# Recurrent stage: one triangular inverse by blocks for both directions, log of beta in the exponent, recurrence steps that follow as chunks end

## The reference, cut to what matters

```python
g    = -exp(a_log) * softplus(a + dt_bias)      # log decay, one per token, head and direction
beta = sigmoid(b)                               # one per token, head and direction
gc   = cumsum(g) within the chunk
gam  = exp(gc_i - gc_j) for j <= i, else 0
a_kk = strict_lower( (k*beta) @ k.T * gam )
u, w = solve (a_kk + I) [u | w] = [v*beta | k*beta*exp(gc)]      # unit lower triangular
a_qk = (q @ k.T) * gam
for every chunk, in order of time:
    v_new = u - w @ state
    o     = (q * exp(gc)) @ state + a_qk @ v_new
    state = state * exp(g_last) + (k * exp(g_last - gc)).T @ v_new
```

## Time and profile before

| | us |
|---|---|
| median of 3 runs (lowest, highest) | 2108.91 (2108.44, 2112.96) |
| the profiled execution's own time | 2110.14 |
| its span in the profile | 2108.3 |
| PE busy | 1998.5 (95%) |
| DVE, ACT, POOL busy | 940.0, 743.6, 614.7 |
| first and last PE record of the gdn stage start at | 212.71, before 546.32 |

### The profile page before, as it was taken

How to read it: one execution, slowest core, us unless ns; L and a number is a source line. 1 busy time by engine, 2 the same in 40 slices (tenths; PEclk the granted TensorE clock), 3 DMA queues, 4 the chain that set the end, 5 groups by cost and what they waited for, 6 DMA issues and landing times.

```text
span 2108.3 us, 25286 instructions
## 1 busy us (share of the span) xinstructions
PE 1998.5 (95%) x10748; PEld 1607.1 (76%) x10748; DVE 940.0 (45%) x1549; ACT 743.6 (35%) x1235; POOL 614.7 (29%) x206
## 2 busy tenths in 40 slices
PE   6998899999999999999999999998999999999997
PEld 3777899999977787778778888887766548766456
DVE  4797455656522221303336403514534664434663
ACT  4674232221433322322233212223343553343551
POOL 2431211222432322334424444442423002423001
PEclk8999799999999999999999999998999999999999
DMA  4121000000233322322222222221312002212001
GB/s 170 60 80 60 1 1 2 2 1 1 95 120 105 106 90 76 111 84 91 89 80 82 98 100 100 100 99 61 130 60 80 1 1 83 90 60 80 1 1 40
DMA packets 29001, 142.01 MB, mean 67 GB/s; under 512 B 2871, under 2 KB 7351, under 8 KB 14808
## 3 DMA queue, kind: packets, MB, share of 16 engines
q1 hardware_dynamic: 18944, 123.27, 16.5%
q10 hardware_dynamic: 9944, 17.12, 2.5%
HBM read 135.13 MB, written 5.24 MB: 67 GB/s over the span
## 4 chain that ended last, share of the span: by engine, by line
PE 86%; DVE 7%; ACT 4%; issue 1%; DMA 0%; POOL 0%; SPq 0%; POOLq 0%; DVEq 0%; ACTq 0%
PE bank L398 48%; PE bank L942 13%; PE bank L599 4%; PE bank L409 3%; PE bank L1800 3%; PE bank L1821 3%; PE bank L1807 2%; DVE WK L868 2%; PE bank L957 2%; PE bank L1275 1%; DVE WK L887 1%; PE bank L1251 1%; PE bank L1749 1%; ACT WK L1930 1%; ACT w_part L356 1%
## 5 line engine op out<-in xcount | busy, mean ns | idle before, releaser
L398 PE MATMUL bank<-x_part,w_part 128*128 128x512 f32 x3360 | 786.7, 394 | 3.5 <-ACT WK L1497 3.0
L398 PEld LDWEIGHTS bank<-x_part,w_part 128*128 128x128 f32 x3360 | 633.1, 189 | 141.5 <-issue 9.0
L2240 POOL TENSOR_TENSOR w_part<-RAW,w_part 128x2048 fp32r<-128x2048 f32 (+1 forms) x90 | 403.3, 4484 | 780.1 <-ACT w_part L356 777.7
L942 PE MATMUL bank<-WK 128*128 128x64 f32 (+1 forms) x2336 | 281.2, 277 | 3.4 <-DVE WK L1088 1.6
L942 PEld LDWEIGHTS bank<-WK 128*128 128x128 f32 x2336 | 275.7, 195 | 4.3 <-DVE WK L1088 1.8
L2240 POOL TENSOR_TENSOR w_part<-WK,w_part 128x2048 fp32r<-128x2048 f32 (+1 forms) x30 | 126.2, 4206 | 376.5 <-ACT w_part L356 376.5
L356 ACT ACTIVATE w_part<-RAW 128x2048 fp32r<-128x2048 f32 (+1 forms) x90 | 166.4, 1850 | 173.9 <-PE bank L398 138.3
L398 PE MATMUL bank<-f_part,w_part 128*128 128x512 f32 x768 | 174.4, 389 | 0.0
L398 PEld LDWEIGHTS bank<-f_part,w_part 128*128 128x128 f32 x768 | 144.2, 188 | 29.9
L868 DVE SCALAR_TENSOR_TENSOR WK<-WK,COL 128x512 f32<-128x512 f32 x96 | 101.7, 1060 | 3.4
L1009 ACT ACTIVATE WK<-bank 128x256 f32<-128x256 f32 x80 | 31.0, 388 | 200.9 <-PE bank L957 200.6
(11 more groups left out here) (257 smaller groups left out, 2372.6 us busy)
## 6 DMA issues: line engine op xcount, KB each, us to landing
RAW<-wts SPq DMA_DIRECT2D x84, 1024.0 KB, 4.8
WK<-wts SPq DMA_DIRECT2D x24, 1024.0 KB, 4.8
WK<-scratch ACTq DMA_DIRECT2D x16, 256.0 KB, 2.7
RAW<-wts SPq DMA_DIRECT2D x6, 512.0 KB, 3.3
WK<-wts SPq DMA_DIRECT2D x6, 512.0 KB, 3.2
scratch<-WK ACTq DMA_DIRECT2D x4, 768.0 KB, 3.3
WK<-xT SPq DMA_DIRECT2D x4, 512.0 KB, 7.1
WK<-xT ACTq DMA_DIRECT2D x1, 2048.0 KB, 11.1
```

The lines of the kernel that those rows point to most:

```text
L398: mm = pe.eng.matmul(b[:, :], W[w][:, k, c:c + P], src[x][k], start=start and k == 0 and n == 0, stop=stop and k == kn - 1 and n == 2)
L942: mul = lambda o, a, b: E.matmul(o, a, b, start=True, stop=True)
L2240: eng.tensor_tensor(low_part(i), raw_part(i), high_part(i).bitcast(F32), ALU.subtract).then_inc(w_split, 1)
```

## The change

Per chunk and half of the heads there is now one unit (8 units) that inverts for both directions at once. `A` holds the sum of the two masked decay matrices times k k', so its lower triangle is the forward direction's and its upper one the backward direction's. The inverse is kept as two half-filled matrices side by side in `RAW`; `p` and `tu` are four matmuls of 128 columns (64 of each direction) for both directions together. The transposed matrix U is mixed from both by an ACT copy (`mixed`) and turned once per level. The last level is 8 matmuls of 64 x 64. Beta is no longer a factor: its logarithm is added in the exponent, and goes with the decay into `A`, `qm` and the scale of the state update.

The units start in the slots `START`, run through 17 phases, and the steps of the recurrence (three phases each: `ks`; `x`; `ds`, `qs`, `ov`) begin when the unit of their chunk has ended, at least 3 slots after the step before. DVE now adds the two directions; POOL has 6 instructions of 128 x 512 for a unit. `RAW` is used as work space, so the first three Z weight pieces are loaded only when parts of it are free.

The diff, cut:

```diff
         def gates_act():
...
-            act.eng.activation(SM[3], GT[:, :, 16:32], ACT.Exp, scale=-1.0).then_inc(*act.did("eb"))
...
         def gates_decay(dve, V):
...
-            V.tensor_scalar(SM[3], SM[3], 1.0, None, ALU.add).then_inc(*dve.did())
-            V.reciprocal(BT, SM[3]).then_inc(*dve.did("beta"))
+            V.tensor_scalar(LNB, GE[:, :, 16:32], -1.0, None, ALU.mult).then_inc(*dve.did("ln_beta"))
...
-        PHASES = 20
-        LAG = (0, 1, 8, 9)
-        LEVELS = range(5, 17)
+        units = [(c, hf) for c in (0, 3, 1, 2) for hf in range(2)]
+        START = (0, 1, 2, 3, 12, 13, 19, 20)
+        INVERSE = 17
...
+        def t_open_of(u, l, h):
+            b = 1 << l
+            return t_view(u, h * P + b, (512 - b, 2), (2 * b, 64 // b), (1, b))
...
+        def begin(s, gi):
+            at_ = START[unit_of[chunk_of(d, s), hf]] + INVERSE
+            return max(at_, begin(s - 1, gi) + 3) if s else at_
         def in_flight():
+            for slot in range(last):
+                for s in range(TT):
+                    for gi in range(4):
+                        if 0 <= slot - begin(s, gi) < 3:
+                            yield "step", slot - begin(s, gi), s, gi
+                for u in range(8):
+                    if 0 <= slot - START[u] < INVERSE:
+                        yield "inverse", slot - START[u], u, None
...
         def gdn_pe():
+            def invert(u, ph):
                 if ph == 0:
+                    for d in range(2):
+                        four(("gr", u, d), ...)
                 elif ph == 3:
+                    four(("kk", u), ...)
+                    four(("qk", u), ...)
                 elif ph == 4:
+                    pe.wait_ge(*at(("a", u)))
+                    four(("p", u, 0), lambda o, h: E.matmul(o, A[:, h, :], split_ident, start=True, stop=True, is_transpose=True), half_of)
+                    if not update:
+                        pe.wait_ge(*at(("t", u, l - 1)))
+                        four(("p", u, l), lambda o, h: mul(o, A[:, h, :], t_open_of(u, l, h)), half_of)
+                        if l == 6:
+                            for d in range(2):
+                                four(("ut", u, 5, d), lambda o, h: E.transpose(o, t_heads(u, d)[:, h, :], ident))
+                        elif l > 1:
+                            pe.wait_ge(*at(("mixed", u, l - 1)))
+                            four(("ut", u, l - 1), lambda o, h: E.transpose(o, UC[:, h, :], ident))
+                    elif l < 6:
+                        pe.wait_ge(*at(("u", u, l - 1)))
+                        pe.wait_ge(*at(("pm", u, l)))
+                        four(("tu", u, l), lambda o, h: mul(o, UC[:, h, :], PB[:, :, h, :]), half_of)
...
         def gdn_act():
+                    for d in range(2):
+                        kept = t_view(u, 0 if d else 513, (P, 4), (2, 64))
+                        A.activation(kept, split_ident[:, d, :].unsqueeze(1).broadcast_to([P, 4, 64]), ACT.Copy)
...
+                        A.activation(uc, t_mixed(u, l + 1), ACT.Copy).then_inc(*act.did(("mixed", u, l)))
...
+            for gi in range(4):
+                act.wait_ge(*at(("pe", ("ov", 2, gi))))
             ahead(upto=first_after_gdn + 1)
         def gdn_pool(low):
+                if ph == 1:
+                    for d in range(2):
+                        pool.wait_ge(*at(("dd", u, d)))
+                        G.tensor_tensor(qm(u, d), qm(u, d), b4(dmask(d)), ALU.add).then_inc(*pool.did(("ddm", u, d)))
+                elif ph == 3:
+                    G.tensor_tensor(A, qm(u, 0), qm(u, 1), ALU.add).then_inc(*pool.did(("decay", u)))
                 elif ph == 4:
+                    pool.wait_ge(*at(("n0", u)))
+                    G.tensor_tensor(t_view(u, 1, (511, 2), (P, 4), (2, 64)), split_ident.unsqueeze(2).broadcast_to([P, 2, 4, 64]),
+                                    product(u), ALU.subtract).then_inc(*pool.did(("t", u, 0)))
+                    G.tensor_tensor(UC, A, b4(pair_mask), ALU.mult).then_inc(*pool.did())
+                    G.tensor_tensor(UC, b4(ident), UC, ALU.subtract).then_inc(*pool.did(("u", u, 0)))
+            low(first_after_gdn)
+            low(first_after_gdn + 1)
...
         @block.sync
+                if first_after_gdn <= i < first_after_gdn + 2:
+                    for u in (4, 5) if i == first_after_gdn else (6, 7):
+                        sp.wait_ge(*at(("pe", ("ut", u, 5, 1))))
```

More of the change, by code:

```diff
@@ new lines, in home, with qm, inverse, a_of @@
+        def home(u, d, part):
+            k = HOME[u, d]
+            if k >= 12:
+                a = 4096 + (k - 12) * 1024 + part * 512
+                return RAW[:, a:a + 512].rearrange("p (h c) -> p h c", h=4)
+            return wk((k * 1024 if k < 10 else 35072 + (k - 10) * 1024) + part * 512, 4, P)
+        def qm(u, d):
+            return home(u, d, 0)
+        def inverse(u, d):
+            return home(u, d, 1)
+        def a_of(u):
+            return home(u, 1, 1)
+        def uc_of(u):
+            return home(u, 0, 1)
@@ new lines, in chunk_out, with product, rhs_of, t_view @@
+        def chunk_out(c, hf):
+            return OTOK[:, c, 4 * hf:4 * hf + 4, :]
+        def product(u):
+            return chunk_out(*units[u]).rearrange("p h (two c) -> p (h two c)", two=2).rearrange("p (two h c) -> p two h c", two=2, h=4)
+        def rhs_of(s, gi):
+            d, hf = groups[gi]
+            if s < 2:
+                return chunk_out(chunk_of(d, s), hf)
+            return qm(unit_of[chunk_of(d, 1), hf], d)
+        def t_view(u, offset, *dims):
+            return bass.AP(tensor=RAW[:, :].tensor, offset=RAW[:, u % 4 * 1024:u % 4 * 1024 + 1].offset + offset,
+                           ap=[list(RAW[:, :].ap[0]), *[list(x) for x in dims]])
@@ new lines, in step @@
+            def step(s, gi, ph):
+                d, hf = groups[gi]
+                c = chunk_of(d, s)
+                u = unit_of[c, hf]
+                tok = slice(c * P, (c + 1) * P)
+                rhs = rhs_of(s, gi)
+                if ph == 0 and s:
+                    pe.wait_ge(*at(("state", s - 1, gi)))
+                    four(("ks", s, gi), lambda o, h: mul(o, KF[:, 4 * hf + h, tok], ST[:, gi, h, :]))
+                elif ph == 1:
+                    pe.wait_ge(*at(("inverse", u, d)))
@@ L989, in gdn_act, with invert @@
             act.stage("gdn")
[L990 to L991 removed]
+            def invert(u, ph):
+                c, hf = units[u]
                 if ph == 0:
[L994 to L1019 removed]
@@ new lines, in step @@
+            def step(s, gi, ph):
+                d, hf = groups[gi]
+                c = chunk_of(d, s)
+                u = unit_of[c, hf]
+                if ph == 1:
+                    nm = ("x", s, gi)
+                    act.wait_ge(*at(("pe", nm)))
+                    if s < TT - 1:
+                        for h in range(4):
+                            k = 8 * d + 4 * hf + h
+                            A.activation(inverse(u, d)[:, h, :], ps(nm)[:, h * P:(h + 1) * P], ACT.Copy, scale=EKD[:, c, k:k + 1])\
+                                .then_inc(*act.did(*([("v2", s, gi)] if h == 3 else [])))
+                    A.activation(rhs_of(s, gi), as4(ps(nm)[:, :]), ACT.Copy).then_inc(*act.did(("x", s, gi), free=nm))
+                elif ph == 2 and s < 2:
+                    act.wait_ge(*at(("pe", ("ov", s, gi))))
+                    A.activation(chunk_out(c, hf), as4(ps(("ov", s, gi))[:, :]), ACT.Copy)\
+                        .then_inc(*act.did(("first", s, gi), free=("ov", s, gi)))
```

371 lines of the change are left out of this document (190 added, 181 removed).

## The result

The changed kernel takes 2014.8 us (median of 4 runs, 2013.86 to 2017.32), the kernel before 2108.8 in the same session: ratio 0.9552, interval 0.9535 to 0.9568. That is 94 us less. Forecast were 76 less (2033), in a range of 2010 to 2069. The profiled execution took 2017.3 us, with a span of 2015.5.

The account below looks back on a forecast made before the run. PE was taken to bound the stage by its number of records. Stage -84.0 (333.6 to 249.6), handover to Z +9.5 and gates -1.8 gave -76.3 us, from the median 2108.9 to 2033; range 2010 to 2069.

Parts of the forecast that it names:

- the last `tu`: Last product of each unit's inverse: 8 multiplications, 16 records, priced at 111.3 ns a record like the rest.
- the fill: Stage start, the first four units waiting on POOL's queue for 43 us: 26 us lost, bounds 17 to 40.
- cheaper than I count: Rival: better overlap at the start, half-cost 64x64 weights (-7), no clock loss before Z: 2010 to 2020; chance 0.12.
- The middle: Stage between its start and its last steps: 10 us of PE stalls between dependent phases, bounds 3 and 30.
- Unit 7: Last inverse unit, its sum queued on POOL behind the unit before and its `A` on DVE: 4.7 us.
- The thin slots: Slots 20 to 36, with only two units in flight: 0.2 us lost a slot, 3 us in all.
- The tail: Last recurrence steps, where PE waits for right sides and the last copy of `x`: 7 us, bounds 4 and 15.
- Into Z: Handover to Z's projection: 5.5 us gap for late rounding plus 4 us at half clock, +9.5; bounds 0 and 12.
- The gates: Before the stage: beta's exponential, its table load and a DVE reciprocal go: -1.8 us, bounds 0 and -5.
- Gapped reads: Rival: moving operands with gaps are slower at 128 columns: +7 us, or +36 giving 2069; chance 0.1.
- Too thin an interleave: Rival: two units in flight stall at each hop and the clock follows down: 2048 to 2067; chance 0.2.
- The lower clock throughout: Rival: PE's clock drops at the stage's start and stays low, up to 180 us added: 2213; chance 0.04.

Follow-up runs that it names:

- the experiment with wide records: The kernel before with its 1536 64-column records of `p` and `tu` made 128 columns wide by reading the same half twice: 2107.9 us, ratio 0.9988.
- The early rounding: The changed kernel with ACT's rounding of the first two Z pieces put ahead of the last step's copies of `x`: 2007.1 us, ratio 0.951.
- the two runs of that edit: The changed kernel with an unused 64-column exponential put back behind the gates' logarithm: one execution 2024.4 us, then a median of 2021.6, ratio 0.9573.

## Why the prediction was right, and where its sizes were off

*Right in its mechanism.* A record costs 111 ns with 64 columns and some 113 with 128, the shared inverse takes 992 of them away, and 992 x 0.1113 = 110.4 us were to go. The PE busy time fell by 108.8, and the experiment with wide records showed the premise alone. The sum was 18 us short of the medians' gain (94 against 76), of which the ledger places 16 in the stage: the overhead there was charged with 43 us and came out at 233.5 - 206.6 = 26.9. Two terms explain it, the price of the last `tu` (9.3) and the clock behind the fill (9), less 2.6 us that the fill itself cost more. By terms:

- *The last `tu`* is the largest: its 128 records were priced at 111 ns with the rest; at 38 they are 9.3 us cheaper. The forecast had this as an item of the "cheaper than I count" rival, at -7.
- *The middle* was charged with 10 us and came out at 233.5 - 206.6 - 19.6 - 5.6 = 1.7. With the 9.3 us of the last `tu` put back it is 11.0, so its own charge was about right, if not in its parts. Unit 7 cost 5.3 instead of 4.7: 1.91 + 1.13 = 3.0 us idle, and 2.3 for 33 records in 6 us at half clock, which the forecast had no term for. The thin slots cost 1 us instead of 3: from 356 to 397 PE does 391 records in 41 us, 48 of them at 38 ns. Other idle time adds 1.8 us, 0.5 of it in the thin slots. The remaining 3 to 4 us I can't place; the width of the records may be 1.5 of them.
- *The fill*: the walk along POOL was right in length (43 us forecast, 44.1 to the last U, with POOL busy for 29.92 of 44.48, or 1.25 us an instruction), and so was its place, POOL's queue and unit 3's lack of cover. The forecast had 17 us of overhead in this walk and 9 behind it, for 15 us at half clock. The walk had 19.6, and behind it there was nothing: from 256 to 299 PE did 396 records in 43.00 us at full clock. *This charge of 9 us is the part of the fill that failed.* The half clock came inside the walk instead, where POOL's queue hides part of it: in the first 4 us of the stage, from 229 to 235.6 and from 249.7 to 256.1. Idle were 11.2 us and not 17, since slower records filled the rest. The rows of before misled here, for the wide version of that kernel went through the same fill without its 13 us at half clock and had its first 200 records done 5.6 us sooner; a part of the stage's -100.1 may be that.
- *The tail*: 5.6 instead of 7. Of the waits on right sides at the starts of steps 2 and 3, one is 1.40 and one 2.27 us, where 3 each were forecast, and 1.6 are the half clock in the last 56 records.
- *Into Z*: 5.33 instead of 5.5 for the gap, and 1.7 instead of 4 for the clock. The early rounding confirms both: it took out the gap and brought Z's projection back to 46.31. The 1.5 us that the ledger has behind Z are not part of it, since the early rounding left them where they were (1517.2 us). The second piece and those behind it caused no wait.
- *The gates*: -1.2 in the ledger instead of -1.8, and the wait fell by 1.53 as worked out (4.74 to 3.21). But the stage began anywhere between 208.6 and 211.5 in kernels that share that part, so a single pair of traces doesn't give this term; the means of four and eight traces above give 2.0. Whether it has a second effect through the clock, the two runs of that edit leave open.
- *The last part of the change*, steps that follow as chunks end, got no price of its own. That was right: without it the kernel was not slower.

*The rivals.* Gapped reads: excluded by experiment, down to about 2% of a record; the changed kernel has 704 of these, an estimated 1.5 us. Too thin an interleave: the stage's middle had one hole, at unit 7. The lower clock throughout: it came back within 7 us each time. Cheaper than I count: its item on the 64x64 weights was true, the one on the clock into Z not, and the time fell inside its case (2010 to 2020), which had been given 0.12. The likeliest case, 2020 to 2048, just missed it. The trace of before had a row that bears on the price of the last `tu`, in a later stage, with weights of 64 columns:

```profile
L1831 PE MATMUL bank<-BASE,WK 128*64 128x128 f32 x256 | 16.7, 273 | 0.0
```

These are fp32 multiplications that write the two halves of the partitions in turn, as the last `tu` does, at 65 ns a record with 128 moving columns. Taken as a bound for the last `tu` it would have put some 6 us of the 9.3 into the sum, and the forecast nearer to its cheaper case.

## What to carry to other kernels

Count PE's fp32 work in records before columns: sharing one 128-wide product between two 64-wide ones halves it, and a product whose weights have only 64 columns is cheap, above all if neighbours write different halves of the partitions. When a pipeline fills through one slow queue, write that queue in the order in which the others need its results; here two deferred instructions a unit and one rounding moved ahead gave 27 us, more than a quarter again on top of a rewrite that gave 94. Before a few microseconds are put down to a cause, see how far the same stretch of code moves between traces in which nothing near it has changed; here it was up to 3 us before the stage and up to 10 behind it. Starting dependent steps as early as possible is no gain by itself: what is left for the end decides how idle the end is.

## What the runs showed of the hardware

- An fp32 multiplication with weights of 128 rows and 64 columns and 64 moving columns costs 56 ns a record, and 38 if neighbours alternate between the partition halves of their output, against 111 for weights of 128 columns with 64 moving columns and some 113 with 128.
- Moving operands of 128 columns, most of them in runs of 2 to 32 floats with gaps, cost about 2% more than those of 64 columns: 1777 records in 200 us at full clock against 1797, with more than half of the records widened.
- Idle times of 3.36, 3.27 and 1.91 + 1.13 us on PE were each followed by 4.5 to 6 us of work at half clock. With 16 to 24 records in front of those waits the clock stayed up, and 80 useless records made the stage shorter, by 6.0 us at these places. Shorter waits went both ways: 2.27 us in the tail, with half clock behind them in four traces and without it in four, and 1.6 to 1.7 us in the fill of the kernel before with 13 us at half clock behind it and, in its wide version, with none.
- What lies behind Z's projection, the same code in all twelve traces, took 1514.4 to 1524.0 us. From 560 us on it ran at a granted clock of 1.00 or 0.96 over 140 us, at equal busy time, and no run here tells what decides.
